# Output-side products of a two-part stack of layers: one 512-column product in place of two 256-column ones

## The reference, cut to what matters

```python
h = h + 0.5 * swiglu(rms_norm(h, ffn1_norm[i]), ffn1_w_in[i], ffn1_w_out[i])  # (silu(g) * u) @ w_out
h = h + m                                # m = (y * h) @ w_out of the mixer
h = h + 0.5 * swiglu(rms_norm(h, ffn2_norm[i]), ffn2_w_in[i], ffn2_w_out[i])
...
y = jnp.concatenate([ya, ym], axis=-1) @ w_out.astype(x.dtype)
return x + y
```

## Time and profile before

| | |
|---|---|
| median of 3 runs | 1516.98 us (1516.81 to 1517.42) |
| profiled execution: its own time | 1516.46 us |
| its span | 1514.7 us |
| TensorE busy | 1473.3 us of the span, 97% |
| VectorE busy | 1051.7 us, 69% |
| ScalarE busy | 770.3 us, 51% |
| products of the output side | 1088 times three |

### The profile page before, as it was taken

One profiled execution on the slowest core, in us unless ns is written; L12 is line 12 of the kernel. 1 busy time (PEld: TensorE's weight loads), 2 busy tenths in 40 slices (PEclk: granted clock), 3 DMA queues, 4 the chain that ended last, 5 costly groups with the idle time before them and its releaser, 6 DMA issues.

```text
span 1514.7 us, 31434 instructions
## 1 busy us (share of the span) xinstructions
PE 1473.3 (97%) x11919; PEld 1454.8 (96%) x11919; DVE 1051.7 (69%) x2005; ACT 770.3 (51%) x1296; POOL 293.9 (19%) x361
## 2 busy tenths in 40 slices
PE   7999999899999999999999999999999999999998
PEld 7999999899999999999999999999999999999898
DVE  6666578766655666557766665898768769976883
ACT  5455448554544545445454544536744453575442
POOL 4111113211102111024221113422240125121000
PEclk9999999999999999999999999999999999999999
DMA  6666754465555556555465555543343554434333
GB/s 203 186 186 201 222 171 132 149 192 180 183 177 184 183 181 191 172 192 168 140 194 174 186 163 172 167 112 108 97 115 101 167 141 140 116 95 125 112 119 119
DMA packets 245276, 239.15 MB, mean 158 GB/s; under 512 B 15160, under 2 KB 244392, under 8 KB 245176
## 3 DMA queue, kind: packets, MB, share of 16 engines
q1 hardware_dynamic: 245176, 237.78, 51.5%
HBM read 236.70 MB, written 1.05 MB: 157 GB/s over the span
## 4 chain that ended last, share of the span: by engine, by line
PE 84%; DVE 11%; ACT 2%; issue 2%; POOL 1%; DMA 0%; SPq 0%; DVEq 0%; ACTq 0%; POOLq 0%
PE bank L565 25%; PE bank L567 25%; PE bank L566 25%; DVE w_lo L1561 3%; DVE work L2023 1%; PE bank L893 1%; PE bank L851 1%; PE bank L833 1%; DVE work L1711 1%; PE bank L762 1%; PE bank L816 1%; PE bank L899 1%; PE bank L909 1%; DVE work L1594 1%; PE bank L832 0%
## 5 line engine op out<-in xcount | busy, mean ns | idle before, releaser
L1561 DVE TENSOR_TENSOR w_lo<-raw,w_hi 128x1024 fp32r<-128x1024 f32 (+1 forms) x456 | 558.3, 1234 | 296.5 <-ACT w_hi L982 296.1
L565 PE MATMUL bank<-x_hi,w_hi 128*128 128x256 f32 (+1 forms) x2480 | 717.1, 289 | 1.7 <-DVE w_lo L1561 1.6
L567 PE MATMUL bank<-x_hi,w_lo 128*128 128x256 f32 (+1 forms) x2480 | 705.7, 285 | 0.0
L566 PE MATMUL bank<-x_lo,w_hi 128*128 128x256 f32 (+1 forms) x2480 | 705.0, 284 | 0.0
L982 ACT CAST w_hi<-raw 128x1024 fp32r<-128x1024 f32 (+1 forms) x456 | 464.4, 1028 | 237.4 <-PE bank L567 227.1
L565 PEld LDWEIGHTS bank<-x_hi,w_hi 128*128 128x128 f32 x2480 | 474.3, 191 | 3.5 <-issue 2.0
L566 PEld LDWEIGHTS bank<-x_lo,w_hi 128*128 128x128 f32 x2480 | 474.4, 191 | 0.9
L567 PEld LDWEIGHTS bank<-x_hi,w_lo 128*128 128x128 f32 x2480 | 474.1, 191 | 0.0
L565 PE MATMUL bank<-y_hi,w_hi 128*128 128x256 f32 (+1 forms) x1088 | 310.6, 285 | 8.3 <-DVE y_lo L1572 8.3
L567 PE MATMUL bank<-y_hi,w_lo 128*128 128x256 f32 (+1 forms) x1088 | 309.7, 285 | 0.0
L566 PE MATMUL bank<-y_lo,w_hi 128*128 128x256 f32 (+1 forms) x1088 | 309.6, 285 | 0.0
(11 more groups left out here) (296 smaller groups left out, 1204.1 us busy)
## 6 DMA issues: line engine op xcount, KB each, us to landing
raw<-in_ffn_w_in_dram SPq DMA_DIRECT2D x176, 512.0 KB, 3.6
raw<-in_w_in_dram SPq DMA_DIRECT2D x100, 512.0 KB, 3.6
raw<-in_ffn_w_out_dram SPq DMA_DIRECT2D x64, 512.0 KB, 4.3
raw<-in_w_out_dram SPq DMA_DIRECT2D x32, 512.0 KB, 3.5
raw<-in_ffn_w_out_dram SPq DMA_DIRECT2D x32, 384.0 KB, 3.1
raw<-in_rec_w_in_dram SPq DMA_DIRECT2D x16, 512.0 KB, 3.5
raw<-in_sg_w_in_dram SPq DMA_DIRECT2D x16, 512.0 KB, 3.6
raw<-in_rec_w_out_dram SPq DMA_DIRECT2D x8, 512.0 KB, 3.5
```

Of the source, the lines that this page charges most:

```text
L565: mm(acc, wh, xh, start=first and j == 0, stop=False)
L566: mm(acc, wh, xl, start=False, stop=False)
L567: i_ = mm(acc, wl, xh, start=False, stop=last and j == n - 1)
L1561: TT(w_lo[:, s, 0:n, :], raw[:, s, 0:n, :], w_hi[:, s, 0:n, :].bitcast(fp32), SUB).then_inc(lo_made, 1)
```

## The change

The upper and lower activations become two halves of one buffer, so that both can be read as one moving operand of two stretches of 256 columns. In the output phases with 256 columns (all of the list above but proj0) the products W_hi X_hi and W_hi X_lo become one product of 512 columns, which fills both halves of the tile's bank. W_lo X_hi goes into the second half. VectorE then adds the second half to `h` by an instruction of its own, waits for it by `link`, and adds the first half as before.

```diff
-        x_hi = sb("x_hi", [P, NC8 * L], fp32r)
-        x_lo = sb("x_lo", [P, NC8 * L], fp32r)
-        y_hi = sb("y_hi", [P, NF * SEQ], fp32r)
-        y_lo = sb("y_lo", [P, NF * SEQ], fp32r)
+        x_both = sb("x_both", [P, 2, NC8 * L], fp32r)
+        y_both = sb("y_both", [P, 2, NF * SEQ], fp32r)
+        x_hi, x_lo = x_both[:, 0, :], x_both[:, 1, :]
+        y_hi, y_lo = y_both[:, 0, :], y_both[:, 1, :]
...
                         wh, wl = (t[:, s, j, m * P:(m + 1) * P] for t in (w_hi, w_lo))
-                        if N == SEQ and wide_x:
-                            xh, xl = (t[:, k * L + META:(k + 1) * L] for t in (hi, lo))
+                        a, b = (k * L + META, (k + 1) * L) if N == SEQ and wide_x else (k * N, (k + 1) * N)
+                        if both:
+                            mm(bank[T % 4][:, 0:2 * N], wh, xs[:, :, a:b], start=first and j == 0, stop=False)
+                            i_ = mm(bank[T % 4][:, N:2 * N], wl, xs[:, 0, a:b], start=False, stop=last and j == n - 1)
                         else:
-                            xh, xl = xview(hi, k, N), xview(lo, k, N)
-                        mm(acc, wh, xh, start=first and j == 0, stop=False)
-                        mm(acc, wh, xl, start=False, stop=False)
-                        i_ = mm(acc, wl, xh, start=False, stop=last and j == n - 1)
+                            mm(acc, wh, xs[:, 0, a:b], start=first and j == 0, stop=False)
+                            mm(acc, wh, xs[:, 1, a:b], start=False, stop=False)
+                            i_ = mm(acc, wl, xs[:, 0, a:b], start=False, stop=last and j == n - 1)
...
-            xs, ys = (x_hi, x_lo), (y_hi, y_lo)
+            xs, ys = x_both, y_both
...
-                    pair(pb + p, ys, N, ready=ready if p == 0 else None)
+                    pair(pb + p, ys, N, ready=ready if p == 0 else None, both=N == SEQ)
...
-                    pair(pb + p, ys, SEQ if narrow else L, ready=SPLITS[f"y_proj{l}"] if p == 0 else None, wide_x=narrow)
+                    pair(pb + p, ys, SEQ if narrow else L, ready=SPLITS[f"y_proj{l}"] if p == 0 else None, wide_x=narrow,
+                         both=narrow)
...
                         wait_tile(pb + p, m)
+                        if N == SEQ:
+                            low = bank[(2 * (pb + p) + m) % 4][:, SEQ:2 * SEQ]
+                            link(STT(out=h[:, c, T0:L], in0=low, scalar=half, in1=h[:, c, T0:L], op0=MUL, op1=ADD))
                         STT(out=h[:, c, T0:L], in0=tile(pb + p, m, N), scalar=half, in1=h[:, c, T0:L], op0=MUL,
                             op1=ADD).then_inc(tile_read, 1)
```

More of the change, by code:

```diff
@@ L544, in unit @@
             def unit(U, k0, n, pair, npair_off, xs, N, first, last, ready, off, tiles=2, wide_x=False,
-                     mid=None):
-                hi, lo = xs
+                     mid=None, both=False):
                 pe.wait_ge(lo_made, U + 1 + off)
@@ L577, in _, with pair @@
             off_half = [0]
-            def pair(pr, xs, N, ready=None, after=None, tiles=2, wide_x=False, mid=None):
+            def pair(pr, xs, N, ready=None, after=None, tiles=2, wide_x=False, mid=None, both=False):
                 us = units_of(pr)
                 for j, (U, k0, n) in enumerate(us):
-                    unit(U, k0, n, pr, 0, xs, N, j == 0, j == len(us) - 1, ready, 0, tiles, wide_x, mid)
+                    unit(U, k0, n, pr, 0, xs, N, j == 0, j == len(us) - 1, ready, 0, tiles, wide_x, mid, both)
                     if after is not None:
                         after(j)
-            xs, ys = (x_hi, x_lo), (y_hi, y_lo)
+            xs, ys = x_both, y_both
             def norm_sum(n, T0):
```

## The result

The changed kernel takes 1522.61 us (median of 7 runs, 1520.73 to 1523.77) against 1516.93 for the kernel before (7 runs): ratio 1.0035, 95% interval 1.0024 to 1.0047. The prediction was 1514.0 with a range of 1507.5 to 1519. So the measured time lies outside the range, and on the other side of no change.

The account below looks back on a forecast made before the run. TensorE was taken as the bound inside the phases, with lateness at handovers. Feed-forward outputs -7.87, mixers +6.20 and proj1 -1.29 gave -2.96 us on 1516.46: 1513.5, so 1514.0 for the median, range 1507.5 to 1519.

Parts of the forecast that it names:

- The product's price: Merged 512-column products on TensorE: 226.3 ns in place of 240.0, saving 13.7 ns per merged pair.
- My dear end of 240: Upper bound for a merged product: each stretch of 256 columns pays its own 13 ns, 240 ns, nothing saved.
- rival C: After rec_out and sg_out, new waits drop the clock to 1.2 GHz, 1.3 us an episode: 1515.3 or 1516.6; chance 0.29.
- The mixers' loop: VectorE and ScalarE's closed loop in rec_out and sg_out takes both additions in full, 5.79 to 6.71 us; sum +6.20.
- Feed-forward outputs: Four output phases, each 2.41 us shorter on TensorE, with stalls of 0.41 (three) and 0.54 behind them; sum -7.87.
- The end: After proj1's last product, the last chunk's extra addition lengthens the kernel by 0.46 us.
- Rival D: Every merged product: two stretches cost as two products, 1525 us; above 230 ns the sum turns positive; chance 0.11.

Follow-up runs that it names:

- experiment 8: Kernel before, products untouched, x chunks spread to 272 columns apart, y_hi moved by 16 columns and y_lo by 32: 1503.01 us, ratio 0.9916.
- experiment 4: Changed kernel with the upper and lower part of each y chunk side by side, one stretch of 512 columns: 1521.23 us, ratio 1.0035.
- experiment 5: Changed kernel with useless products ahead of TensorE's waits for chunks 6 and 7 in in02 and in12: 1518.61 us, ratio 1.0017.
- experiment 2: Kernel before with one more linked addition per tile (times zero) in rec_out and sg_out only, products untouched: 1522.84 us, ratio 1.0043.
- experiment 7: Kernel before with two more linked additions per tile (times zero) in rec_out and sg_out: 1532.8 us, ratio 1.0106.
- experiment 1: Changed kernel, but rec_out and sg_out keep three products and one addition: 1513.34 us, ratio 0.9978.
- experiment 9: Changed kernel's merged products with the addresses of experiment 8, mixers with three products: 1503.87 us, ratio 0.9920.
- experiment 10: Kernel of experiment 8 with 16 more columns between y_hi and y_lo, so y_lo lies 48 columns from where it was: 1502.52 us, ratio 0.9910.
- experiment 6: Kernel before with one more linked addition per tile (times zero) in all output phases of 256 columns, products untouched: 1524.66 us.

## Why the prediction was wrong, and where it was right

**The product's price: wrong, and the first cause.** The step that failed is "If that stays, 512 columns cost 213.3 + 13.0 = 226.3 ns". The forecast group was 226.3 + 120.0 = 346.3 ns; it takes 353.4. With the narrow product left at 120.0 the wide one costs 233.4, and by the starts of out02 it is 236.3, with 117.0 for the narrow one: beside its columns it carries 20 to 23 ns, not 13. I had two points, 256 and 272 columns, and read an extra of equal size as a cost per product, when two points so close can't part a cost per product from one per column; and the 272 point came from another layout, when experiment 8 shows that addresses alone move the distance between starts by 2 ns. Cost: 4 x (2.41 - 1.17) = 5.0 us in the outputs and 1.0 in proj1. My dear end of 240 was kept for two stretches, and experiment 4 shows that stretches are not the matter. The Trainium skill ("TensorE: Matmul & The Clock Gate", "Back-to-back issue gap") gives the isolated gap at the full clock as the columns over 2.4 plus about 2.5 ns. That was farther off: 20 to 23 here.

**The clock: put at nothing in the sum, and the second cause; rival C, under-priced.** The forecast had no fall in its sum, and C counted 1.3 us an episode, at most 2.6 in all. Chunk 7's product starts at 303.03 and 765.84 after. Counted from the start of rec_out and sg_out in each kernel (268.23 and 734.92 after, 268.64 and 733.57 before) it is 2.18 and 3.06 us later than before; the phases lost 3.83 and 5.52. The remaining 1.65 and 2.46, together 4.1, are the clock's, and experiment 5 gave back 3.95 of them by phases. I took 14 products at the low level from the kernel before; behind sg_out there were more, and the norm's sum on top.

**The mixers' loop: right.** Serial, closed, without slack, every addition in full: experiments 2 and 7. The forecast was 2.67 and 3.53 us, and it came to 2.18 and 3.06 (against a rec_out of 29.28 us, as in experiments 1 and 2, the first would be 1.56; the clock's share does not depend on it). The loop grew by 0.75 and not 0.92, because the two `w_lo` of a pair took 2.37 us and no longer 2.54. The first of them runs beside GpSimd's sum of squares (L1422 before, L1423 after), before for 0.33 us (755.77 to 756.10) and after for 0.15 (759.70 to 759.85). That this makes the difference is a guess that no run tested.

**Feed-forward outputs: nearly right.** Forecast 0.41, 0.41, 0.41 and 0.54; it was 0.55, 0.35, -0.08 and 0.56. The stall at chunk 7 itself was 0.26 us (in sg_ab the product at 683.94 starts 0.38 after its neighbour and not 0.12). In sg_ab it was made good within the phase: the wait of 0.2 us for GpSimd's sum of squares that the kernel before has there is gone.

**The end: right.** VectorE's last addition starts 0.78 us after the last product and not 0.32: 0.46.

**Together:** -4.68 + 1.38 + 9.35 - 0.70 + 0.46 = 5.8 of the 6.2 us between the two spans (in01 is 0.2 longer too). Put against the forecast of -2.96: the product's price adds 6.0, the clock 4.1, and the stalls came out 1.0 smaller in the mixers and 0.4 behind the feed-forward outputs, which makes the same 5.8. With the price and these stalls alone the time would have been about 1518.6, slower than before but just inside the range; the clock took it out. Rival D's turning point, 230 ns for the wide product, was right: at 233 the sum had the other sign already (1.7 us without the clock), and the clock took it past what is still no change.

**Open:** what sets the cost beside the columns. It depends on where the moving operand starts and, it seems, on how many columns it has; experiments 8 to 10 show sizes and no mechanism. A merged group also has one weight load fewer than three products, and no run changed the length with the loads kept, so the 6.6 ns can't be put down to the length alone. A shift also moves the buffers behind it, the weights being ahead of them and unmoved.

## What to carry to other kernels

Don't extrapolate a product's price to twice its length from two lengths 6% apart; if a few ns decide, try the long product first, and try the operand's start address before any rewrite of the products. Before an instruction is added to an engine that is "69% busy", look for a loop of that engine with a second one whose period is already that of the bound: there it counts in full. And a wait put on TensorE costs more than itself if the clock falls behind it; here filling the waits with useless products gave some 4 us back.

## What the runs showed of the hardware that was not expected

- Products of 256 columns start 120.0 ns apart when the chunks are 256 columns apart from an aligned start, and 117.8 (62.19 us over 528 products) when y_hi is shifted by 16 columns and y_lo by 32 or 48 (experiments 8 and 10). With the x chunks 272 columns apart as well it is 13 us over the kernel.
- A group of a 512-column and a 256-column product takes 353.4 ns, 33 beside its 320.0 of columns, whether the wide operand is one stretch or two; three products of 256 carry 40.
- Waits far shorter than the 4.25 us of the earlier trace rows were followed by the 1.2 GHz level: 2.01 us behind sg_out, and 0.32 and 1.24 behind rec_out with three products between. Others of the same size were not, in the profiled executions: 1.38 and 1.24 (experiment 2), 0.85 and 1.24 behind rec_out (experiment 4), a single 1.49 (experiment 5). And 1.40 and 1.23 (experiment 6) were, where 1.38 and 1.24 had not been. The waits' lengths alone don't decide it.
